# Order of the wide and narrow products inside a weight unit of the gated feed-forward blocks

## The chip, the cores and the metric

One Trainium2 chip, one core of it. The metric is the device time of one execution of the whole program in microseconds. The kernel before takes 1206.65 us (median of 3 runs, 1206.61 to 1206.96).

## What is computed

A chain of two small models on 256 tokens of width 1024, all in 32-bit floats. The part that the change touches is the gated feed-forward block (`swiglu`), which occurs four times, with a hidden width of 2816:

```python
D_FF = 2816
def swiglu(x, w_gu, w_down):
    gate, up = jnp.split(x @ w_gu, 2, axis=-1)
    return (jax.nn.silu(gate) * up) @ w_down

# layer of type A; the layer of type B has the same two feed-forward blocks
x = x + 0.5 * swiglu(rms_norm(x, ffn1_norm[l]), ffn1_w_gu[l], ffn1_w_down[l])
...
x = x + 0.5 * swiglu(rms_norm(x, ffn2_norm[l]), ffn2_w_gu[l], ffn2_w_down[l])
```

The program calls the four blocks a1, a2 (the two of layer A), b1 and b2 (the two of layer B). Everything else (a first model with attention and pooling, a gated delta rule, latent attention, norms) is left as it is.

## The kernel before

Activations lie transposed, 128 features on the partitions and 256 tokens in a row, so x is KC = 8 chunks of 128x256. Weights stream in from memory once, in slabs of two units. A unit of the up stage is 128 output features: eight pieces of 128x128, one for each chunk k. Each weight and each activation is split in a high and a low part: ScalarE writes `w_hi` from `raw` (`split_hi`, L576), VectorE writes `w_lo` = raw - w_hi (`split_lo`, its subtraction is L1120), and a product is high x high + low x high + high x low. Both rings hold four units (RING = 4).

In the up stage a unit is done by `project_halves` (L2104 on). For chunk k it issues two matmuls: one with the stationary piece `w_hi` and 512 moving columns, the high and the low part of the activations side by side (L2110, into all 512 columns of the unit's bank), and one with the stationary piece `w_lo` and the 256 high columns (L2112, added to the lower half of the same bank). So a unit is 8 pairs of a 512-column and a 256-column product, 16 matmuls, in the order 512, 256, 512, 256 and so on. Each matmul has a weight load of its own. TensorE waits at the unit's start for the semaphore of `w_lo` (`unit_begin`, L2087) and for a free bank (`bank_of`); the last matmul of the unit counts `unit_used` up (`unit_end`). That one signal frees the ring place for ScalarE (`slot` in the scalar block) and releases the readers of the bank: ScalarE copies the upper half out (`take_low`, L772), VectorE adds the lower half (`both_halves`, L1451), multiplies by the norm, and `silu`, gate product and a new split for the down stage follow (L785, L1484, L792).

`ffn(which)` holds the up stage. Its function `turn` does four units; the first turn of each block is written out with its own waits (`first` is given), and a loop on the engine (`Fori`) does the rest: 10 turns of 4 units in each of the four blocks (for b1 two pairs of units were done ahead). The down stage after it has its own code (`down`, L2419 and L2421) in the same 512, 256 order. The first turn of a2, b1 and b2 goes through `enter` (L2129, L2131). The trace shows 1328 matmuls each of L2110 and L2112.

SyncE issues the weight transfers by slab, four slabs ahead (RAW = 4), with waits on the ring.

Of the kernel before, what the change touches and what calls it, by code (L numbers as in the profile page):

```python
# [16 lines left out]
KC = D // P  # L17
SEQ = 256
# [139 lines left out]
def program(nc, dram, out):  # L158
    with ExitStack() as ctx:
# [7 lines left out]
        xs, _ = place("xs", at + 32, [P, KC, 2, SEQ], F32R)  # L167
        xs_hi, xs_lo = xs[:, :, 0], xs[:, :, 1]
# [5 lines left out]
        w_hi, at = place("w_hi", at, [P, RING, UNIT], F32R)  # L174
        w_lo, at = place("w_lo", at, [P, RING, UNIT], F32R)
# [180 lines left out]
        xh_ready, xg_ready = sem("xh_ready"), sem("xg_ready")  # L356
# [61 lines left out]
        def piece(tensor, u, b, n=1):  # L418

            return tensor[:, u % RING, b * P:(b + n) * P]  # L420
# [1653 lines left out]
        def _(pe):  # L2074
            def bank_of(t, off=0):

                if t >= 4:
                    pe.wait_ge(evac, t - 3 + off)
                return main[t % 4]
# [21 lines left out]
                    ins = triple(dst, piece(w_hi, u, k), piece(w_lo, u, k), hi[:, k], lo[:, k], k == 0, k == KC - 1)  # L2101
                unit_end(ins)

            def project_halves(u, bank, off=0, first=None):  # L2104

                unit_begin(u, off)
                for k in range(KC):
                    if first is not None:
                        pe.wait_ge(xg_ready, first + k + 1)
                    pe.matmul(bank[:, :], piece(w_hi, u, k), xs[:, k], start=k == 0, stop=k == KC - 1,  # L2110
                              skip_group_check=True)
                    ins = pe.matmul(bank[:, 0:SEQ], piece(w_lo, u, k), xs_hi[:, k], start=False, stop=k == KC - 1,  # L2112
                                    skip_group_check=True)
                unit_end(ins)

            def enter(u, banks, parts, first, late=1, norm=None, ready=xg_ready):
# [137 lines left out]
            for i in range(11):  # L2254
                ins = pe.matmul(side[1][:, 0:P], acc[:, 0:P], acc[:, 0:P], start=True, stop=True)
            ins.then_inc(warmed, 1)
            bank = side[2]
            pe.wait_ge(small_lo, 1)
            for k in range(KC):
                pe.wait_ge(xg_ready, k + 1)  # L2260
                w = slice(k * 8, k * 8 + P)
                ins = triple(bank[:, 0:TOK], wf_hi[:, w], wf_lo[:, w], xg_hi[:, k, :], xg_lo[:, k, :],
                             k == 0, k == KC - 1)
# [3 lines left out]
            t0 = FIRST_TILE["in1"]  # L2267
            for u in range(40):
# [6 lines left out]
                if u == POOL_AT:  # L2275
                    pe.wait_ge(pool_split, 1)
                    for j in range(2):
                        unit_begin(first_unit("w_pool") + j)
                        for i in range(2):
                            g = 2 * j + i  # L2280
                            ins = triple(pool_tile(g), piece(w_hi, first_unit("w_pool") + j, i),
                                         piece(w_lo, first_unit("w_pool") + j, i),
                                         pool_hi[:, g, :], pool_lo[:, g, :], True, True)
                        unit_end(ins)
                if 8 <= u < 12:

                    j = u - 8
# [4 lines left out]
                    for i, tok in enumerate((0, META, META + P)):  # L2292
                        for kk in range(2):
                            k = 2 * j + kk
                            x_t = slice(tok, tok + P)
                            ins = triple(main[(t0 + 8 + i) % 4][:, :], xg_hi[:, k, x_t], xg_lo[:, k, x_t],
                                         piece(w_hi, u, 4 * kk, 4), piece(w_lo, u, 4 * kk, 4),
                                         k == 0, k == KC - 1)
                    unit_end(ins)
                else:  # L2300
                    first = 0 if 4 <= u < 8 or 16 <= u < 20 else META
                    bank = bank_of(t0 + (u if u < 8 else u - 1))
# [3 lines left out]
                    if u == 0:  # L2306
                        pe.wait_ge(half_lo, 1)
                        for k in range(KC):
                            if k == KC // 2:
                                unit_begin(u)  # L2310
                            ins = triple(bank[:, 0:SEQ], piece(w_hi, u, k), piece(w_lo, u, k),
                                         xg_hi[:, k, META:TOK], xg_lo[:, k, META:TOK], k == 0, k == KC - 1)
# [3 lines left out]
                if u == 4:  # L2316

                    pe.wait_ge(rstd_ready, 1)
                    for j, (tok, n) in enumerate(((0, META), (META, P), (META + P, P))):
                        ins = pe.matmul(side[0][0:n, j:j + 1], rstd[:, tok:tok + n], ident[:, 0:1],  # L2320
                                        start=True, stop=True)
# [13 lines left out]
            t0, u0 = FIRST_TILE["up"], first_unit("w_up")  # L2335
# [50 lines left out]
            def ffn(which):  # L2386
                f, u0, t0 = FFNS.index(which), first_unit("w_gu_" + which), FIRST_TILE["gu_" + which]

                def turn(i, first=None):
                    if first is not None and which != "a1":  # L2390
                        enter(u0, [bank_of(t0 + j) for j in range(2)], (xs_hi, xs_lo) if which == "b2" else (xs,), first,
                              2 if which == "b2" else 1, None if which == "b2" else FFN_NORM[which])
                    for j in range(2 if first is not None and which != "a1" else 0, 4):
                        if which == "b2" and first is not None:
                            project(u0 + j, bank_of(t0 + j)[:, 0:SEQ], xs_hi, xs_lo,
                                    within=(KC - 2, lambda: norm_sum(FFN_NORM[which])) if j == 2 else None)
                        else:
                            project_halves(u0 + j, bank_of(t0 + j, i * 4), i * 4, first if j == 0 else None)
                        if first is not None and which == "a1" and j == 0:
                            norm_sum(FFN_NORM[which])  # L2400

                if which != "b1":
                    turn(0, XG0["ffn_" + which])
                with pe.Fori(0 if which == "b1" else 1, (FT - FFN_FIRST[which]) // 2) as i:
                    turn(i)
                u0, t0 = first_unit("w_down_" + which), FIRST_TILE["down_" + which]

                def down(m, i=0, joined_parts=True):
                    bank = bank_of(t0 + m, i * 4)
                    for j in range(2):  # L2410
                        u = u0 + 2 * m + j
                        pe.wait_ge(h_ready, f * FT + FT // 2 + j * (FT // 2 - 2))
                        unit_begin(u, i * 8)
                        for b in range(FT // 2):
                            k = j * (FT // 2) + b
                            if k >= FT - 2:
                                pe.wait_ge(h_ready, f * FT + k + 1)
                            if joined_parts:
                                pe.matmul(bank[:, :], piece(w_hi, u, b), h_both[:, :, k, :], start=k == 0,  # L2419
                                          stop=k == FT - 1, skip_group_check=True)  # L2420
                                ins = pe.matmul(bank[:, 0:SEQ], piece(w_lo, u, b), h_hi[:, k, :], start=False,  # L2421
                                                stop=k == FT - 1, skip_group_check=True)
                            else:
                                ins = triple(bank[:, 0:SEQ], piece(w_hi, u, b), piece(w_lo, u, b),
                                             h_hi[:, k, :], h_lo[:, k, :], k == 0, k == FT - 1)
                        unit_end(ins)

                if which == "b2":
                    for m in range(KC):
                        down(m, joined_parts=m < KC - 1)  # L2430
                else:
                    with pe.Fori(0, 2) as i:
                        for m in range(4):
                            down(m, i)
# [588 lines left out]
```

## Time and profile before

| | |
|---|---|
| median of the runs | 1206.65 us |
| the profiled execution | 1206.3 us, its span (first to last instruction) 1204.5 us |
| TensorE busy | 1194.0 us, 99% of the span, 7964 matmuls |
| TensorE weight loads | 1100.7 us, 91% |
| VectorE / ScalarE / GpSimd busy | 935.3 / 728.0 / 88.4 us |
| L2110, the 512-column products of the up stages | 1328, 461.1 us |
| L2112, the 256-column products of the up stages | 1328, 374.5 us |
| read from memory | 207.86 MB, 173 GB/s over the span |

Matmuls overlap in the pipeline: a 512-column one is shown 390 ns long and a 256-column one 282 ns, though the next one starts well before these have passed. What TensorE needs for a matmul is therefore the distance from its start to the next one's start, called its step below. It is read from the timeline, best over many matmuls.

### The profile page before, as it was taken

To read this page: it belongs to the slowest core of one execution; us is meant where nothing else is said; L and a number is where in the kernel's file an instruction comes from. 1 tells how busy PE (TensorE), PEld (TensorE's weight loads), DVE (VectorE), ACT (ScalarE), POOL (GpSimd) and SP (SyncE) were. 2 spreads that over 40 slices of the span, in tenths; PEclk is the share of its full clock that TensorE was granted. 3 is DMA by queue.
4 is the path that set the end of the run, shared out by engine and by line. 5 is a ranking of instruction groups with operands and counts; after the bars stand their busy time and mean duration, and the time that the engine had idled before them with its cause. 6 is when DMAs were issued, how large, how long until landed. Compare 5 with 4: busy or idle time off the path is not lost.

```text
span 1204.5 us, 22407 instructions
## 1 busy us (share of the span) xinstructions
PE 1194.0 (99%) x7964; PEld 1100.7 (91%) x7964; DVE 935.3 (78%) x1620; ACT 728.0 (60%) x1197; POOL 88.4 (7%) x104
## 2 busy tenths in 40 slices
PE   9999999999999999999999999999999999999998
PEld 8899999988888999999888889988888999888887
DVE  7576788988876789778888867888876777888853
ACT  6455656666654589467666556666654566666642
POOL 4851000000000001610000000000000000000000
PEclk9999999999999999999999999999999999999999
DMA  8444555655664445104555743555664423555730
GB/s 325 179 141 152 210 208 175 208 186 205 206 234 153 140 167 163 66 36 167 186 205 178 256 164 121 205 193 180 227 233 141 139 100 126 190 203 181 257 124 36
DMA packets 47993, 209.87 MB, mean 174 GB/s; under 512 B 3351, under 2 KB 4773, under 8 KB 43445
## 3 DMA queue, kind: packets, MB, share of 16 engines
q1 hardware_dynamic: 46720, 204.96, 48.2%
q10 hardware_dynamic: 1204, 4.01, 0.9%
q8 instruction: 41, 0.67, 0.2%
q14 instruction: 28, 0.22, 0.0%
HBM read 207.86 MB, written 1.10 MB: 173 GB/s over the span
## 4 chain that ended last, share of the span: by engine, by line
PE 92%; DVE 4%; ACT 2%; issue 1%; DMA 0%; DVEq 0%; ACTq 0%
PE main L2110 25%; PE main L2112 13%; PE main L2419 13%; PE main L2083 8%; PE main L2084 8%; PE main L2085 8%; PE main L2421 7%; DVE w_lo L1120 2%; DVE cy L1574 1%; PE side L2216 1%; PE main L2578 1%; PE main L2462 1%; PE side L2190 1%; PE main L2753 1%; PE main L2755 1%
## 5 line engine op out<-in xcount | busy, mean ns | idle before, releaser
L1120 DVE TENSOR_TENSOR w_lo<-raw,w_hi 128x1024 fp32r<-128x1024 f32 (+3 forms) x365 | 467.0, 1287 | 8.3 <-ACT w_hi L576 7.2
L2110 PE MATMUL main<-xs,w_hi 128*128 128x512 f32 x1328 | 461.1, 390 | 1.3 <-DVE w_lo L1120 0.8
L576 ACT ACTIVATE w_hi<-raw 128x1024 fp32r<-128x1024 f32 (+2 forms) x363 | 402.4, 1110 | 79.1 <-PE main L2085 59.0
L2112 PE MATMUL main<-xs,w_lo 128*128 128x256 f32 x1328 | 374.5, 282 | 0.0
L2110 PEld LDWEIGHTS main<-xs,w_hi 128*128 128x128 f32 x1328 | 249.2, 188 | 54.0 <-DVE w_lo L1120 1.8
L2112 PEld LDWEIGHTS main<-xs,w_lo 128*128 128x128 f32 x1328 | 251.0, 189 | 0.0
L2419 PE MATMUL main<-h_both,w_hi 128*128 128x512 f32 x682 | 236.6, 390 | 0.0
L2421 PE MATMUL main<-h_both,w_lo 128*128 128x256 f32 x682 | 192.3, 282 | 0.0
L2419 PEld LDWEIGHTS main<-h_both,w_hi 128*128 128x128 f32 x682 | 128.0, 188 | 26.8
L2421 PEld LDWEIGHTS main<-h_both,w_lo 128*128 128x128 f32 x682 | 128.9, 189 | 0.0
L2083 PE MATMUL main<-xs,w_hi 128*128 128x256 f32 x368 | 105.5, 287 | 0.4 <-DVE w_lo L1120 0.3
L2084 PE MATMUL main<-xs,w_lo 128*128 128x256 f32 x368 | 102.8, 279 | 0.0
L2085 PE MATMUL main<-xs,w_hi 128*128 128x256 f32 x368 | 102.6, 279 | 0.0
L2083 PE MATMUL main<-xg,w_hi 128*128 128x256 f32 (+1 forms) x288 | 83.8, 291 | 0.0
L2084 PE MATMUL main<-xg,w_lo 128*128 128x256 f32 (+1 forms) x288 | 81.0, 281 | 0.0
L2085 PE MATMUL main<-xg,w_hi 128*128 128x256 f32 (+1 forms) x288 | 81.0, 281 | 0.0
L1451 DVE TENSOR_TENSOR hid<-main,hid 128x256 f32<-128x256 f32 x84 | 35.6, 424 | 52.7 <-ACT hid L772 52.7
L772 ACT ACTIVATE hid<-main 128x256 f32<-128x256 f32 x84 | 32.1, 382 | 71.4 <-PE main L2112 71.3
L594 ACT ACTIVATE xs<-x,par 128x256 fp32r<-128x256 f32 (+1 forms) x48 | 23.9, 507 | 77.6 <-DVE x L1421 67.1
L2083 PEld LDWEIGHTS main<-xs,w_hi 128*128 128x128 f32 x368 | 69.2, 188 | 1.0 <-issue 0.7
L2084 PEld LDWEIGHTS main<-xs,w_lo 128*128 128x128 f32 x368 | 69.2, 188 | 0.1
L2085 PEld LDWEIGHTS main<-xs,w_hi 128*128 128x128 f32 x368 | 69.2, 188 | 0.0
(478 smaller groups left out, 1884.7 us busy)
## 6 DMA issues: line engine op xcount, KB each, us to landing
raw<-in_w_gu_a SPq DMA_DIRECT2D x44, 1024.0 KB, 5.1
raw<-in_w_gu_b SPq DMA_DIRECT2D x44, 1024.0 KB, 5.1
raw<-in_w_down_a SPq DMA_DIRECT2D x16, 1408.0 KB, 6.0
raw<-in_w_down_b SPq DMA_DIRECT2D x16, 1408.0 KB, 6.0
raw<-in_w_in SPq DMA_DIRECT2D x15, 1024.0 KB, 7.6
raw<-in_w_in_a SPq DMA_DIRECT2D x13, 1024.0 KB, 5.2
raw<-in_w_gates SPq DMA_DIRECT2D x4, 1024.0 KB, 5.2
raw<-in_w_up SPq DMA_DIRECT2D x4, 1024.0 KB, 5.2
```

The source lines that it names most:

```text
L576: act.activation(w_hi[:, u % RING, 0:n], raw[:, s % RAW, u % 2, 0:n], ACT.Copy).then_inc(hi_ready, 1)
L594: act.activation(dst, src, ACT.Copy, scale=g).then_inc(xh_ready, 1)
L772: act.activation(dst, main[(t0 + n) % 4][:, SEQ:2 * SEQ], ACT.Copy).then_inc(low_half, 1)
L1120: return dve.tensor_tensor(dst, src, hi.bitcast(F32), ALU.subtract)
L1451: dve.tensor_tensor(dst, main[(t0 + n) % 4][:, 0:SEQ], dst, ALU.add).then_inc(evac, 1)
L2083: pe.matmul(dst, a_hi, b_hi, start=first, stop=False)
L2084: pe.matmul(dst, a_lo, b_hi, start=False, stop=False)
L2085: return pe.matmul(dst, a_hi, b_lo, start=False, stop=last)
L2110: pe.matmul(bank[:, :], piece(w_hi, u, k), xs[:, k], start=k == 0, stop=k == KC - 1, skip_group_check=True)
L2112: ins = pe.matmul(bank[:, 0:SEQ], piece(w_lo, u, k), xs_hi[:, k], start=False, stop=k == KC - 1, skip_group_check=True)
L2419: pe.matmul(bank[:, :], piece(w_hi, u, b), h_both[:, :, k, :], start=k == 0, stop=k == FT - 1, skip_group_check=True)
L2421: ins = pe.matmul(bank[:, 0:SEQ], piece(w_lo, u, b), h_hi[:, k, :], start=False, stop=k == FT - 1, skip_group_check=True)
```

## The change

`project_halves` gets a parameter `group`. The chunks are walked in groups: in a group first all 512-column products are issued, then all 256-column ones. With group 1 the order is the one before. Block a1 gets 2, a2 gets 8 (the whole unit), b1 gets 4, b2 gets 1; the turn that is written out with `first` keeps 1. The number of matmuls, their operands, all waits and signals stay.

```diff
-            def project_halves(u, bank, off=0, first=None):
+            def project_halves(u, bank, off=0, first=None, group=1):
 
                 unit_begin(u, off)
-                for k in range(KC):
-                    if first is not None:
-                        pe.wait_ge(xg_ready, first + k + 1)
-                    pe.matmul(bank[:, :], piece(w_hi, u, k), xs[:, k], start=k == 0, stop=k == KC - 1,
-                              skip_group_check=True)
-                    ins = pe.matmul(bank[:, 0:SEQ], piece(w_lo, u, k), xs_hi[:, k], start=False, stop=k == KC - 1,
-                                    skip_group_check=True)
+                for k0 in range(0, KC, group):
+                    for k in range(k0, k0 + group):
+                        if first is not None:
+                            pe.wait_ge(xg_ready, first + k + 1)
+                        pe.matmul(bank[:, :], piece(w_hi, u, k), xs[:, k], start=k == 0, stop=k == KC - 1,
+                                  skip_group_check=True)
+                    for k in range(k0, k0 + group):
+                        ins = pe.matmul(bank[:, 0:SEQ], piece(w_lo, u, k), xs_hi[:, k], start=False, stop=k == KC - 1,
+                                        skip_group_check=True)
                 unit_end(ins)
...
-                            project_halves(u0 + j, bank_of(t0 + j, i * 4), i * 4, first if j == 0 else None)
+                            project_halves(u0 + j, bank_of(t0 + j, i * 4), i * 4, first if j == 0 else None,
+                                           {"a1": 2, "a2": KC, "b1": 4, "b2": 1}[which] if first is None else 1)
```

## Rows read from the trace of the kernel before

**Rows 1.** The page: busy time of the engines, and TensorE's granted clock in 40 slices.
```profile
PE 1194.0 (99%) x7964; PEld 1100.7 (91%) x7964; DVE 935.3 (78%) x1620; ACT 728.0 (60%) x1197; POOL 88.4 (7%) x104
...
PEclk9999999999999999999999999999999999999999
```

**Rows 2.** The page: the chain that ended last, shares by engine and by line.
```profile
PE 92%; DVE 4%; ACT 2%; issue 1%; DMA 0%; DVEq 0%; ACTq 0%
PE main L2110 25%; PE main L2112 13%; PE main L2419 13%; PE main L2083 8%; PE main L2084 8%; PE main L2085 8%; PE main L2421 7%; DVE w_lo L1120 2%; DVE cy L1574 1%; PE side L2216 1%; PE main L2578 1%; PE main L2462 1%; PE side L2190 1%; PE main L2753 1%; PE main L2755 1%
```

**Rows 3.** Busy time by stretch, in the loops of a1, a2, b1, b2; clock, DMA last.
```profile
core 0: us, PE busy (x) PEld busy (x) DVE busy (x) ACT busy (x) POOL busy (x), PEclk, DMA share, GB/s
225.00:340.00 115.00, 115.00 (x665) 101.94 (x665) 97.81 (x170) 73.83 (x126) 0.00 (x0) 1.00 0.59 204
575.00:685.00 110.00, 110.00 (x637) 97.53 (x636) 94.03 (x162) 70.84 (x120) 0.00 (x0) 1.00 0.58 205
775.00:885.00 110.00, 110.00 (x637) 97.49 (x636) 92.09 (x157) 70.56 (x120) 0.00 (x0) 1.00 0.58 205
1030.00:1140.00 110.00, 110.00 (x637) 97.53 (x636) 94.35 (x161) 72.00 (x121) 0.00 (x0) 1.00 0.58 205
```

**Rows 4.** Waits between engines, 225 to 340 us: total us, times, longest.
```profile
ACT hid L772 <- PE main L2112: 17.2, 18, 1.0
DVE hid L1451 <- ACT hid L772: 13.5, 19, 0.8
ACT h_both L792 <- DVE hid L1484: 13.1, 21, 0.8
ACT gate_n L772 <- PE main L2112: 7.2, 18, 0.4
```

**Rows 5.** TensorE's timeline in block a1, pairs: start us, length us, instruction.
```profile
300.04 0.39 PE L2110 MATMUL main<-xs,w_hi 128*128 128x512 f32 x1
300.27 0.28 PE L2112 MATMUL main<-xs,w_lo 128*128 128x256 f32 x1
300.39 0.39 PE L2110 MATMUL main<-xs,w_hi 128*128 128x512 f32 x1
...
340.60 0.39 PE L2110 MATMUL main<-xs,w_hi 128*128 128x512 f32 x1
```

**Rows 6.** TensorE's timeline, first model: 512-column products in one row.
```profile
35.63 0.39 PE L2083 MATMUL main<-w_hi,xg 128*128 128x512 f32 x1
35.86 0.39 PE L2084 MATMUL main<-w_hi,xg 128*128 128x512 f32 x1
...
38.88 0.40 PE L2085 MATMUL main<-w_lo,xg 128*128 128x512 f32 x1
39.11 0.40 PE L2083 MATMUL main<-w_hi,xg 128*128 128x512 f32 x1
39.35 0.40 PE L2084 MATMUL main<-w_hi,xg 128*128 128x512 f32 x1
...
52.16 0.40 PE L2085 MATMUL main<-w_lo,xg 128*128 128x512 f32 x1
```

**Rows 7.** TensorE's timeline: first and last of 47 256-column products, activations moving.
```profile
429.59 0.28 PE L2084 MATMUL main<-xs,w_lo 128*128 128x256 f32 x1
...
434.96 0.28 PE L2085 MATMUL main<-xs,w_hi 128*128 128x256 f32 x1
```

**Rows 8.** TensorE's timeline: first and last of 47 256-column products, weights moving.
```profile
212.90 0.28 PE L2084 MATMUL main<-w_hi,mem_lo 128*128 128x256 f32 x1
...
218.35 0.28 PE L2085 MATMUL main<-w_lo,mem_hi 128*128 128x256 f32 x1
```

**Rows 9.** TensorE's weight loads beside the pair of Rows 5: start us, length us.
```profile
300.05 0.19 PEld L2112 LDWEIGHTS main<-xs,w_lo 128*128 128x128 f32 x1
300.27 0.19 PEld L2110 LDWEIGHTS main<-xs,w_hi 128*128 128x128 f32 x1
300.39 0.19 PEld L2112 LDWEIGHTS main<-xs,w_lo 128*128 128x128 f32 x1
```

**Rows 10.** TensorE's timeline in block a2: the wait for w_lo inside the up stage.
```profile
571.11 0.28 PE L2112 MATMUL main<-xs,w_lo 128*128 128x256 f32 x1
572.22 0.50 PE L2110 MATMUL main<-xs,w_hi 128*128 128x512 f32 x1 [0.83 <-DVE w_lo L1120]
```

## The prediction

> **What bounds the kernel now.** I read the page first: TensorE is busy for 99% of the span, at the full granted clock in all 40 slices [rows 1]. The chain that ended last is TensorE for 92%, and the two lines that the change reorders, L2110 and L2112, are 25% and 13% of it, the largest share of any two lines [rows 2]. Busy time is a weak witness for TensorE, since its matmuls overlap, so I read the loops of the four blocks by stretch: TensorE has no idle time at all in them, VectorE is busy for 97.81 of 115 us, ScalarE for 73.83, and the DMA engines for 0.59 of the time, at 204 GB/s; b2's stretch looks like the others [rows 3]. The waits say the same from the other side: in the loop of a1 ScalarE and VectorE wait for L2112's end and for each other, and no wait of TensorE is among the four longest [rows 4]. The only stall of TensorE of that kind that I found inside an up stage's loop is one in a2, 0.83 us, for the first `w_lo` after the entry [rows 10]. So the time of an up stage is the number of matmuls times their steps, and whatever the new order does to a step goes straight to the end.
>
> The step now: from 300.04 to 340.60 us lie 117 pairs of a 512-column and a 256-column product [rows 5], 40.56 us, so 346.7 ns for a pair. The single starts give about 0.23 us for the 512 and 0.12 us for the 256 [rows 5]. This average over 117 pairs includes fourteen unit boundaries, so a boundary adds nothing that shows.
>
> **The change, part by part.** *Matmuls, weight loads, signals.* None is added or taken away. The waits stand where they stood, at the unit's start; `unit_used` still comes from the last matmul of the unit, a 256-column one as before. The queues of SyncE, ScalarE, VectorE and GpSimd are not touched, and no DMA is moved. The pieces of `w_lo` are read later in the unit, but they are still waited for at its start, so nothing is won at the stall of 0.83 us [rows 10]. The upper half of the bank is finished earlier, by up to seven 256-column products in a2, but its reader waits for `unit_used` and gains nothing. Cost of all this: nothing. If a step does grow, VectorE and ScalarE only wait longer; if it shrinks, VectorE has 115 - 97.81 = 17 us of cover in that stretch, 15% [rows 3], far more than a step can shrink.
>
> *Neighbours.* What does change is which product stands beside which. In a group of g chunks, g - 1 times a 512-column product is followed by a 512-column one instead of by a 256, and g - 1 times a 256 is followed by a 256 instead of by a 512. Call one such couple a join. A unit has 4 joins in a1 (four groups of 2), 7 in a2 (one group of 8), 6 in b1 (two groups of 4) and none in b2. Each block has 10 turns of 4 units in its loop, 40 units, so 40 x (4 + 7 + 6) = 680 joins among 960 pairs of 120 units. The time moves by 680 times the difference between (step of a 512 among 512s + step of a 256 among 256s) and 346.7 ns.
>
> *A 256 among 256s.* 47 of them in a row, with the activations `xs` moving as here, start from 429.59 to 434.96 us: 5.37 us over 46 steps, 116.7 ns [rows 7]. With the weights as the moving operand it is 5.45 over 46, 118.5 ns [rows 8]. I take 116.7, since the operands are those of the change; the other is the upper end.
>
> *A 512 among 512s.* The change's own case, `xs` moving in a row of 512s, is not in the trace. The nearest is the first model's row of 72, where the weights move and the activations are stationary: from 35.63 to 52.16 us are 71 steps, 16.53 us, 232.8 ns [rows 6]. It is not even: two steps from 38.88 to 39.35 take 0.47 us, 235 ns each, and the first one, 35.63 to 35.86, takes 0.23 [rows 6]. A 256-column product loses 118.5 - 116.7 = 1.8 ns when the weights are what moves [rows 7, 8]; I take that off once and get 231.0 ns for `xs` moving. The upper end is 235. The lower end is further away. In the pairs 256 more columns cost 0.23 - 0.12 = 0.11 us [rows 5], so 512 columns by themselves are worth about 220 ns, and if standing in a row took away all that comes on top, 220 would be the step. Nothing excludes it, so it stays an end of the range. The loads say little either way: each starts with the matmul ahead of its own (300.27 beside the matmul of 300.27), is shown 0.19 us long, and the next matmul starts 0.12 us after it began [rows 5, 9]; beside a 512 a load has more room than that, so two 512s in a row can't wait for a load.
>
> *The sum.* 231.0 + 116.7 = 347.7 ns against 346.7, so +1.0 ns for a join and 680 x 1.0 = +0.7 us. The profiled execution took 1206.3 us (its span 1204.5 and 1.8 around it), which gives 1207.0; the median of the runs lies 0.35 us higher, so 1207.35 there. By block that is +0.16 us in a1, +0.28 in a2 and +0.24 in b1, too little to be seen in any of them except by counting steps. With the ends: 232.8 + 116.7 = 349.5 gives +1.9 us (1208.6), which is the case that the row of 512s holds as it stands; 228 + 116.7 = 344.7, where a 512 keeps the step that it has in the pairs (346.7 less 118.5 is 228.2), gives -1.4 us (1205.3). These three are one case to me: no order matters by more than 3 ns for a join.
>
> A measurement of this kernel can tell about 0.2% from no change, 2.4 us here, which is 3.5 ns for a join.
>
> **The rivals.** *A, the row of equal widths runs free.* If what a 512-column step has on top of its columns comes from the change of width, it goes in a row: 220 + 116.7 = 336.7, -10.0 ns for a join, -6.8 us, 1199.9. For it speaks that a 256 among 256s is 1 or 2 ns shorter than beside a 512 [rows 5, 7]; against it, that the 72 equal 512s of the first model never get near 220 [rows 6]. For the same end there is a rule of the Trainium skill, page "TensorE: Matmul & The Clock Gate", section "Back-to-back issue gap": columns divided by 2.4 GHz plus 2.5 ns at the full clock. That would make 215.8 and 109.2, 325.0 for a pair, and by it the sum for 680 joins would be -14.8 us; the pairs here take 346.7, so this trace does not agree with it for the order of before, and for the order of after it is one more reason to leave A a chance.
>
> *B, the row of equal widths is the slower rhythm.* In the mixed order the stretch 512, 256 takes less than the sum of its parts from the two uniform rows (346.7 against 232.8 + 116.7 = 349.5). If that is a matter of rhythm, that a load beside a 256 and the reading of the next moving columns catch up with each other only when widths alternate, then the first 512s of a group settle, as in the first model, from 0.23 to 0.235 [rows 6], and the 256s behind them don't gain: 235 + 118.5 = 353.5, +6.8 ns for a join, +4.6 us, 1211.2. It counts as slower from 3.5 ns for a join. For it speaks the uneven row of 512s, whose later steps are longer; against it that such a row has another moving operand, and that 256s in a row do gain. The Trainium skill says in the same page, section "Step-by-step: what each phase is for", that loading the next weights does not steal read bandwidth from the running matmul; by that no order could cost anything and B would be +0. The trace can't show it, as no matmul here runs without a load beside it.
>
> *C, nothing happens.* The step of a pair is set by its 768 columns and two loads, whatever stands beside them: 346.7 as before, 1206.65. It can't be told from the forecast in the total, only in the steps.
>
> **How the numbers follow.** The forecast and C lie together between 1205.3 and 1208.6 and hold 0.62. A, in full or in part, has 0.18: only a step of a kind that the trace does not have would bring it. B, in full or in part, has 0.20. The range reaches into both, to leave about one in ten outside at each end: below, 1203.5 is -4.6 ns for a join, a 512 at 225.4 with a 256 at 116.7 (680 x -4.6 = -3.1 us from the median); above, 1210.5 is +5.7 ns for a join (+3.9 us). The predicted time is 1207.35, given as 1207.4. Chances: faster by over 0.2% 0.18, within it 0.62, slower 0.20.
>
> **What the changed kernel's profile would show.** Right, if the pairs in b2's loop still take 346.7 ns; if in a2's loop (from about 575 us) a unit of eight 512s and eight 256s takes 2.77 to 2.79 us, with starts of the 512s 0.23 us apart and of the 256s 0.12; if TensorE still has no idle time in the loops and the waits on L2112's end by ScalarE are as long as now. A would show 512s 0.22 us apart and a2's loop about 2.8 us shorter, most of all blocks, as it has 7 of the 17 joins of each set of units. B would show steps of 0.235 and more, and a2 longer by about 1.9 us. Wrong altogether would be the count of joins if the loss or gain were not in the proportion 4 : 7 : 6 between a1, a2 and b1, or if b2 moved too; wrong would also be the claim on signals if a stall of TensorE appeared at a unit's start that isn't there now.

## The result and the profile after

The changed kernel takes 1208.85 us (median of 19 executions, 1208.4 to 1209.47) against 1206.55 for the kernel before (19 executions, 1206.33 to 1206.96): +2.3 us, ratio 1.0020, 95% interval 1.0013 to 1.0026. The profiled execution took 1208.72 us, its span is 1206.9.

The page of the changed kernel, busy time, chain by engine, and the two lines (L2111 and L2114 are the L2110 and L2112 of before):

```profile
PE 1196.0 (99%) x7964; PEld 1098.0 (91%) x7964; DVE 935.7 (78%) x1620; ACT 728.2 (60%) x1197; POOL 88.3 (7%) x104
...
PE 91%; DVE 5%; ACT 2%; issue 1%; DMA 1%; DVEq 0%; SPq 0%; ACTq 0%
...
L2111 PE MATMUL main<-xs,w_hi 128*128 128x512 f32 x1328 | 395.8, 393 | 1.3 <-DVE w_lo L1120 0.8
L2114 PE MATMUL main<-xs,w_lo 128*128 128x256 f32 x1328 | 261.5, 280 | 0.0
```

The same two lines on the page of the kernel before:

```profile
L2110 PE MATMUL main<-xs,w_hi 128*128 128x512 f32 x1328 | 461.1, 390 | 1.3 <-DVE w_lo L1120 0.8
L2112 PE MATMUL main<-xs,w_lo 128*128 128x256 f32 x1328 | 374.5, 282 | 0.0
```

Beside [rows 1, 2] and these nearly all is the same: as many instructions, as much idle time ahead of the two lines (1.3 and 0.0 us). Their busy time falls from 461.1 and 374.5 to 395.8 and 261.5 us, which is no gain: matmuls of one line that overlap are merged when they are neighbours. The page doesn't tell where 2.3 us went. The stretches inside the four loops do, by their counts (columns as in [rows 3]):

```profile
225.00:340.00 115.00, 115.00 (x666) 101.43 (x665) 97.79 (x170) 73.64 (x127) 0.00 (x0) 1.00 0.58 203
575.00:685.00 110.00, 110.00 (x632) 95.64 (x631) 93.30 (x159) 69.84 (x121) 0.00 (x0) 1.00 0.58 205
777.00:887.00 110.00, 110.00 (x629) 95.52 (x629) 91.18 (x157) 69.81 (x119) 0.00 (x0) 1.00 0.58 204
1032.00:1142.00 110.00, 110.00 (x636) 97.55 (x635) 94.32 (x162) 71.97 (x122) 0.00 (x0) 1.00 0.58 205
```

TensorE is busy without a gap in all of them, at the full granted clock, before and after. But in 110 us it starts 632 matmuls in a2 and 629 in b1, where it started 637 before [rows 3]; in a1 (115 us) and b2 they are 666 and 636, within one of the 665 and 637 of before. So the loss lies in a2 and b1, in the steps and not in waits. TensorE's timeline gives the steps. Where matmuls of one line follow each other, a row merges them; its start is that of the first of them. First a1 (groups of 2), then a2 (8), b1 (4) and b2 (1):

```profile
300.22 0.62 PE L2111 MATMUL main<-xs,w_hi 128*128 128x512 f32 x2
300.67 0.40 PE L2114 MATMUL main<-xs,w_lo 128*128 128x256 f32 x2
...
340.43 0.62 PE L2111 MATMUL main<-xs,w_hi 128*128 128x512 f32 x2
...
600.51 2.03 PE L2111 MATMUL main<-xs,w_hi 128*128 128x512 f32 x8
602.38 1.09 PE L2114 MATMUL main<-xs,w_lo 128*128 128x256 f32 x8
...
662.11 2.03 PE L2111 MATMUL main<-xs,w_hi 128*128 128x512 f32 x8
...
800.63 1.09 PE L2111 MATMUL main<-xs,w_hi 128*128 128x512 f32 x4
801.57 0.63 PE L2114 MATMUL main<-xs,w_lo 128*128 128x256 f32 x4
...
860.84 1.09 PE L2111 MATMUL main<-xs,w_hi 128*128 128x512 f32 x4
...
1100.07 0.39 PE L2111 MATMUL main<-xs,w_hi 128*128 128x512 f32 x1
...
1133.69 0.39 PE L2111 MATMUL main<-xs,w_hi 128*128 128x512 f32 x1
```

- a1: 58 groups of two, 116 pairs, in 340.43 - 300.22 = 40.21 us: 346.6 ns a pair. Nothing lost.
- a2: 22 units, 176 pairs, in 662.11 - 600.51 = 61.60 us: 350.0 ns a pair. Eight 512s take 1.87 us; over the whole loop, by the trace's unrounded starts, a 512 takes 233.3 and a 256 116.7.
- b1: 43 groups of four, 172 pairs, in 860.84 - 800.63 = 60.21 us: 350.1 ns a pair.
- b2: 97 pairs in 33.62 us: 346.6 ns.

320 pairs of a2 and 320 of b1 at 3.33 ns more each make +2.13 us of the 2.3. The rest, about 0.2 us, lies ahead of the loops of a2 and b1 in the profiled execution: the wait in a2 of [rows 10] ends at 572.40 instead of 572.22, before any group of more than two has run. The first 222 us of the program, which no experiment here touches, vary by as much and more: over the traces of this document the first up-stage product of a1 starts between 221.35 and 222.17 us. The row in a2 shows the same wait as before:

```profile
572.40 2.13 PE L2111 MATMUL main<-xs,w_hi 128*128 128x512 f32 x8 [0.83 <-DVE w_lo L1120]
```

### The profile page after: what moved, and what is told of

Same layout as the page of the kernel before. It is cut to its first block, busy times and chain, and to the rows that moved or that the text cites. A ratio compares the mean times of both kernels' runs of the same rounds, so it can differ in the third digit from the quotient of the medians.

```text
span 1206.9 us, 22407 instructions
## 1 busy us (share of the span) xinstructions
PE 1196.0 (99%) x7964; PEld 1098.0 (91%) x7964; DVE 935.7 (78%) x1620; ACT 728.2 (60%) x1197; POOL 88.3 (7%) x104
## 4 chain that ended last, share of the span: by engine, by line
PE 91%; DVE 5%; ACT 2%; issue 1%; DMA 1%; DVEq 0%; SPq 0%; ACTq 0%
PE main L2111 25%; PE main L2114 13%; PE main L2422 13%; PE main L2083 8%; PE main L2084 8%; PE main L2085 8%; PE main L2424 7%; DVE w_lo L1120 2%; DVE cy L1574 1%; PE side L2218 1%; PE main L2581 1%; PE main L2465 1%; PE side L2192 1%; PE main L2756 1%; PE main L2758 1%
## 5 line engine op out<-in xcount | busy, mean ns | idle before, releaser
L2111 PE MATMUL main<-xs,w_hi 128*128 128x512 f32 x1328 | 395.8, 393 | 1.3 <-DVE w_lo L1120 0.8
L2114 PE MATMUL main<-xs,w_lo 128*128 128x256 f32 x1328 | 261.5, 280 | 0.0
L2111 PEld LDWEIGHTS main<-xs,w_hi 128*128 128x128 f32 x1328 | 229.7, 188 | 34.5 <-DVE w_lo L1120 1.8
L2114 PEld LDWEIGHTS main<-xs,w_lo 128*128 128x128 f32 x1328 | 221.2, 188 | 24.3
L2084 PE MATMUL main<-xs,w_lo 128*128 128x256 f32 x368 | 102.9, 280 | 0.0
L2083 PEld LDWEIGHTS main<-xs,w_hi 128*128 128x128 f32 x368 | 69.2, 188 | 1.0 <-issue 0.7
L2084 PEld LDWEIGHTS main<-xs,w_lo 128*128 128x128 f32 x368 | 69.3, 188 | 0.1
L2085 PEld LDWEIGHTS main<-xs,w_hi 128*128 128x128 f32 x368 | 69.2, 188 | 0.0
```

The source lines that it names most:

```text
L2083: pe.matmul(dst, a_hi, b_hi, start=first, stop=False)
L2084: pe.matmul(dst, a_lo, b_hi, start=False, stop=False)
L2085: return pe.matmul(dst, a_hi, b_lo, start=False, stop=last)
```

## The experiments

Two theories stood against each other after this. J is the prediction's: every couple of equal neighbours costs a little. R, for rhythm (a sequence of steps that repeats through a whole loop): only the order of widths matters, groups of two cost nothing and longer rows cost the same 3.3 ns for every pair, however many changes of width are left. `ORDER` is a table that I put in the place of the argument `group`; W is a 512-column product, n a 256-column one; runs(2, 2, 2, 2) is four groups of two, runs(8) one of eight.

**e1_two_all**

```diff
-{"a1": 2, "a2": KC, "b1": 4, "b2": 1}[which] if first is None else 1
+{"a1": 2, "a2": 2, "b1": 2, "b2": 2}[which] if first is None else 1
```

> Groups of two in the loops of all four blocks (the changed kernel has them in a1 only). In the changed kernel's trace the loop of a1 keeps 346.7 ns for a pair of a 512- and a 256-column product, the loops of a2 (rows of eight) and b1 (rows of four) take 350. Theory R (rhythm: only long rows of one width are slow, groups of two are free): 0.0 us, ratio 1.000 to the kernel before, 346.7 ns for a pair in all four loops. Theory J (each couple of equal neighbours costs, as in the prediction): 160 units x 4 joins = 640 joins; with the 2.14 us that a2 and b1 lost spread over the 680 joins of the changed kernel, 3.15 ns each, +2.0 us, ratio 1.0017.

Measured: median 1208.44 against 1206.55, ratio 1.0013 (1.0004 to 1.0022; the ratios are those on record and can differ by a few ten-thousandths from the quotient of the medians), but the eleven executions don't stand around that median: four took 1206.5 to 1206.9 and seven took 1208.4 to 1208.9. The profiled one was of the first kind and had all four loops at 346.7, as R says. J's +2.0 us fits the second kind only by chance, as e8 below shows.

**e2_eight_all**

```diff
-{"a1": 2, "a2": KC, "b1": 4, "b2": 1}[which] if first is None else 1
+{"a1": KC, "a2": KC, "b1": KC, "b2": KC}[which] if first is None else 1
```

> One group of eight (all 512-column products of a unit, then all its 256-column ones) in the loops of all four blocks, 160 units. Theory R: every pair costs 350.0 instead of 346.7 ns, 160 x 8 x 3.35 = +4.3 us over the kernel before, ratio 1.0036, the same loss of 1.07 us in each block. Theory J: 160 x 7 = 1120 joins x 3.15 = +3.5 us, ratio 1.0029. A theory by which the loss is nothing but the spread between traces: under +1 us.

Measured: 1211.04 against 1206.55 us, ratio 1.0038 (1.0024 to 1.0051), +4.5 us, five executions within 0.45 us. R gave +4.3, J +3.5; the interval of the ratio, some +2.9 to +6.2 us, holds both, so the steps decide. J's 3.15 ns for a join would be 349.4 ns a pair. In the trace the loops of a1 and b1 take 350.0 ns a pair and those of a2 and b2 350.8, which makes 2 x 1.07 + 2 x 1.33 = +4.8 us; the profiled execution, the longest of the five at 1211.39, is 4.8 above the median of before. So double the dose costs double, and a loop can stand a little above 350 too.

**e3_patterns**

```diff
+ORDER = {
+    "a1": runs(3, 3, 2),
+    "a2": [(kind, (k + 4 * (kind == "n")) % KC) for k in range(KC) for kind in "Wn"],
+    "b1": pattern("WWWWnnWWnnWWnnnn"),
+    "b2": [("W", k) for k in range(KC)] + [("n", k) for k in reversed(range(KC))],
+}
```

> Four orders in one kernel, one for each block's loop; what is read is the step in each loop, W a 512-column product, n a 256-column one. a1: groups of 3, 3 and 2. a2: widths alternate as before, but the 256-column product behind chunk k is that of chunk (k + 4) mod 8, so weights and moving columns of neighbours are no longer of the same chunk. b1: WWWWnnWWnnWWnnnn, rows of four only at the ends of the unit. b2: a row of eight 512s, then the eight 256s in reverse order of chunks. Theory R (the widths' order alone decides, groups over two are slow): a1 2800 ns for a unit if three is already too long, else between 2773 and 2800; a2 2773; b1 between, as its middle is groups of two; b2 2800. Theory O (what counts is that a chunk's two products stand together, the same 256 moving columns twice): a2 2800, b2 2800. Theory J: a1 5 joins, 2790; a2 none, 2773; b1 8 couples of 512s and 256s less the mixed ones, about 5 joins, 2790.

Measured, per pair in each loop: a1 350.8 ns, a2 346.7, b1 348.3, b2 350.8 (a unit is eight times that: 2807, 2773, 2787, 2807). The total was 1209.67 us. TensorE's timeline of a2 in this kernel, two pieces of it:

```profile
600.17 0.39 PE L2140 MATMUL main<-xs,w_hi 128*128 128x512 f32 x1
600.40 0.28 PE L2143 MATMUL main<-xs,w_lo 128*128 128x256 f32 x1
...
660.49 0.39 PE L2140 MATMUL main<-xs,w_hi 128*128 128x512 f32 x1
```

174 pairs in 60.32 us, 346.7 ns, though the two neighbours are of chunks four apart. Theory O (the chunk's two products must stand together) falls, and J with it: a1 has 5 joins and loses as much as b2 with 7. Rows of three are already too long, and the group of two beside them doesn't run free either: its 512s take 231 to 234 ns. In b1 a 512 takes 233.3 ns in the row of four that opens the unit and 228.0 in the groups of two in the middle; the unit loses 13 ns, half of what a unit of long rows loses, on average 348.3 a pair.

**e4_one_width**

```diff
+ORDER = {
+    "a1": by_chunk("W", "L"),   # L: w_lo against all 512 columns
+    "a2": by_row("W", "L"),
+    "b1": by_chunk("h", "n"),   # h: w_hi against the 256 high columns
+    "b2": by_row("h", "n"),
+}
```

> Sixteen products of one width in each unit, to separate width from weights. a1: both products of a chunk 512 columns wide, loads of w_hi and w_lo taking turns (this adds the low x low part). a2: the same, first the eight with w_hi, then the eight with w_lo. b1: only 256 columns for w_hi too (this leaves out the high x low part), w_hi and w_lo taking turns. b2: the same, eight w_hi and then eight w_lo. Theory R (width alone): a1 and a2 both 233.3 ns a product, b1 and b2 both 116.7. Theory H (the faster step of the order before comes from w_hi and w_lo taking turns at the load): a1 near 228.3 and b1 near 116 or less, a2 233.3 and b2 116.7. The total is of no interest: a1 and a2 are longer by 16 x 233.3 - 2773 = 960 ns a unit, some 77 us for both, and b1 and b2 shorter until the weights' transfer is what they wait for.

The timeline of its a1, where `w_hi` and `w_lo` take turns at 512 columns:

```profile
299.66 0.40 PE L2132 MATMUL main<-xs,w_hi 128*128 128x512 f32 x1
299.90 0.39 PE L2132 MATMUL main<-xs,w_lo 128*128 128x512 f32 x1
...
302.46 0.40 PE L2132 MATMUL main<-xs,w_hi 128*128 128x512 f32 x1
```

Twelve steps in 2.80 us, 233.3 ns, and over the whole loop 233.3 as well, in a2 the same. Theory H falls: it is not the turn of `w_hi` and `w_lo` at the load that gives 228 ns, but the turn of widths. It also gives the number that the prediction lacked: with `xs` moving a 512 among 512s takes 233.3 ns. In b1 and b2 TensorE waited for VectorE's `w_lo` at unit after unit, so their mean step says nothing; with the steps that hold a wait left out, a 256 takes 117.1 ns where `w_hi` and `w_lo` take turns (b1) and 117.2 in rows (b2), so at 256 columns too the turn of the weights makes no difference. The total, 1249.91 us, is that of more work and not a comparison.

**e8_two_again**, the kernel of e1 unchanged, to catch the other kind of execution.

> The kernel with groups of two in all four blocks once more, unchanged. Its executions fell in two clusters, 1206.5 to 1206.9 and 1208.4 to 1208.9, and the profile that was taken was of the first (1206.7), with 346.7 ns for a pair in all four loops. If the groups of two can run in the slower rhythm too, a profiled execution near 1208.7 shows loops with more than 346.7 ns for a pair: two of the four loops at 350.0 (2 x 1.07 = +2.1 us), or all four at 348.3. If the second cluster comes from somewhere else (a start, a stall), all four loops stay at 346.7 and the 2.1 us lie elsewhere. A profile of the first cluster again leaves it open.

The profiled execution was of the second kind, 1208.58 us. Median of eight 1208.62 against 1206.5, ratio 1.0015 (1.0004 to 1.0027); one of the eight was at 1206.88, the others from 1208.4 on. TensorE's timeline, first in a1, then in a2:

```profile
300.07 0.62 PE L2135 MATMUL main<-xs,w_hi 128*128 128x512 f32 x2
300.53 0.40 PE L2138 MATMUL main<-xs,w_lo 128*128 128x256 f32 x2
300.76 0.62 PE L2135 MATMUL main<-xs,w_hi 128*128 128x512 f32 x2
...
572.26 0.73 PE L2135 MATMUL main<-xs,w_hi 128*128 128x512 f32 x2 [0.83 <-DVE w_lo L1141]
...
574.48 0.63 PE L2135 MATMUL main<-xs,w_hi 128*128 128x512 f32 x2
574.96 0.40 PE L2138 MATMUL main<-xs,w_lo 128*128 128x256 f32 x2
575.19 0.64 PE L2135 MATMUL main<-xs,w_hi 128*128 128x512 f32 x2
...
672.71 0.64 PE L2135 MATMUL main<-xs,w_hi 128*128 128x512 f32 x2
```

and the same stretch in the profiled execution of e1, which took 1206.68 us:

```profile
574.02 0.62 PE L2135 MATMUL main<-xs,w_hi 128*128 128x512 f32 x2
574.48 0.40 PE L2138 MATMUL main<-xs,w_lo 128*128 128x256 f32 x2
574.72 0.62 PE L2135 MATMUL main<-xs,w_hi 128*128 128x512 f32 x2
...
668.32 0.62 PE L2135 MATMUL main<-xs,w_hi 128*128 128x512 f32 x2
```

It is the same program on the same data, and a2's loop runs in another rhythm, from its first group to its last: 139 groups, 278 pairs, in 98.23 us are 353.3 ns a pair in e8, and 136 groups, 272 pairs, in 94.30 us are 346.7 in e1. The other three loops take 346.7 in both. 320 x 6.67 = 2.13 us, which is the distance of the two clusters. So a steady order of products can run in more than one steady rhythm, and a loop keeps the one it is in.

Where the rhythm is picked isn't shown. The two traces of a2 differ from the first group behind the wait of 0.83 us on: behind the first two 512s, e8's steps are 120, 115, 238, 234 ns and again, while e1's come to 117, 120, 227, 229 within two groups. TensorE enters b2's loop behind idle time as well, and those of a1 and b1 without any. From the trace of the kernel before, at b2's first product:

```profile
1024.07 0.49 PE L2110 MATMUL main<-xs,w_hi 128*128 128x512 f32 x1 [0.49 <-DVE gate_n L1249]
```

An order has been seen at two rates in one and the same loop in a2 alone: groups of two at 346.7 and 353.3, and rows of eight at 350.0 in the changed kernel and 350.8 in e2 and e11.

**e5_columns_rows** and **e6_columns_turns** cut the wide products to 320, 384, 448 and 480 columns, one width for each block, once in rows of eight and once taking turns.

```diff
+e5: ORDER = {"a1": by_row("W", "n", 320), "a2": by_row("W", "n", 384), "b1": by_row("W", "n", 448), "b2": by_row("W", "n", 480)}
+e6: ORDER = {"a1": by_chunk("W", "n", 320), "a2": by_chunk("W", "n", 384), "b1": by_chunk("W", "n", 448), "b2": by_chunk("W", "n", 480)}
```

> The row of eight in each loop, with the wide products cut to fewer columns: 320 in a1, 384 in a2, 448 in b1, 480 in b2 (this leaves out a part of the high x low sum, so it is only for reading steps). In rows, 256 columns take 116.7 ns and 512 take 233.3. Theory P (in a row a column costs the same however many there are, 0.456 ns): 145.8, 175.0, 204.2, 218.8 ns. Theory F (full rate of one column in 1/2.4 ns and a fixed part of 20 ns at 512): 153, 180, 207, 220 ns; it does not fit the 116.7 of 256 columns, where the fixed part would be 10. Theory Q (the step only takes certain lengths): steps from 256 to 512 in jumps, two neighbouring column counts alike.

> The order of the kernel before (wide and narrow taking turns), with the wide products cut as in the kernel for rows: 320 columns in a1, 384 in a2, 448 in b1, 480 in b2. At 512 columns the pair takes 346.7 ns, 3.3 less than 233.3 + 116.7 of the uniform rows. Theory R (any mix of widths saves about 3 ns a pair over rows): pairs of 259, 288, 317.5 and 332 ns, if rows go in proportion. Theory S (only 512 beside 256 happens to fit): the saving differs from width to width or is gone, pairs of 262.5, 291.7, 320.8, 335.4.

Mean steps of a wide product and of a pair in the loops, from the unrounded starts, over 270 to 320 products of each kind (512: the changed kernel's a2 and the kernel before). With 320 and 384 columns TensorE waited for `w_lo` at unit starts, in both orders alike (a1's products span 102.47 us in both kernels, a2's 101.18 and 101.19). The steps that hold such a wait are left out; at 384 columns some are hard to tell from the others, so its pairs are good to about 0.5 ns:

| columns | wide, in rows | wide, taking turns | pair, in rows | pair, taking turns |
|---|---|---|---|---|
| 320 | 146.4 | 145.7 | 263.8 | 263.3 |
| 384 | 175.0 | 174.5 | 292.1 | 291.7 |
| 448 | 203.8 | 202.7 | 320.8 | 320.0 |
| 480 | 216.8 | 217.2 | 334.2 | 333.3 |
| 512 | 233.3 | 228.3 | 350.0 | 346.7 |

Theory P is within 1% in rows, F is out by 4 to 5% at 320 and Q falls too: the steps grow all the way. For the turns R is wrong and S right, its pairs within 0.7%: from 320 to 480 columns taking turns saves 0.4 to 0.9 ns, and the 3.3 ns are there only at 512. The two totals, single executions of 1162.32 and 1161.81 us, differ by 0.5 us, as the table would have it for b1 and b2 (2 x 320 x 0.8 ns); in the two traces each of these loops differs by 0.25 to 0.27 us. So "taking turns is faster" is no rule; the full width of 512 beside 256 is the case that gains by it.

**e7_two_banks**

```diff
+TWO_UNITS = {
+    "a1": [(kind, j, k) for k in range(KC) for j in range(2) for kind in "Wn"],
+    "a2": [(kind, j, k) for k in range(KC) for kind in "Wn" for j in range(2)],
+    "b1": [(kind, j, k) for kind in "Wn" for k in range(KC) for j in range(2)],
+    "b2": None,
+}
```

> Two units at a time, so that neighbours can go to different banks of the accumulator: a1 W n of one unit, W n of the other, chunk by chunk; a2 W of both, then n of both; b1 rows of sixteen W and sixteen n, banks taking turns; b2 as before. Theory B (the time over the columns' own comes from adding into the same bank again and again): with banks changing from product to product a2 and b1 fall, towards 325 to 335 ns for a pair. Theory R (widths alone): a1 346.7, a2 346.7 (groups of two), b1 350, whatever the bank, b2 346.7.

The total is 1398.52 us: two units are freed together and TensorE waits for `w_lo` in every couple of units, two of its waits stand below, and the granted clock falls to half in stretches behind them (0.958 on average). That is the cost of the edit, not of banks. The steps inside can still be read; the timeline of b1, banks changing from product to product:

```profile
970.73 3.76 PE L2158 MATMUL main<-xs,w_hi 128*128 128x512 f32 x15 [2.19 <-DVE w_lo L1146]
974.34 2.03 PE L2161 MATMUL main<-xs,w_lo 128*128 128x256 f32 x16
976.20 0.40 PE L2158 MATMUL main<-xs,w_hi 128*128 128x512 f32 x1
978.78 5.31 PE L2158 MATMUL main<-xs,w_hi 128*128 128x512 f32 x15 [2.18 <-DVE w_lo L1146]
```

Sixteen 256s take 1.87 us by the unrounded starts, 116.7 each. Inside the row of 512s one starts at 971.30 and one at 973.87, eleven steps in 2.57 us, 233.6 each. With a new bank for each product both steps are those of one bank, and Theory B falls. Over all of b1's loop at the full granted clock, steps with a wait left out, a pair takes 349.6 ns (Theory R 350, Theory B 325 to 335), a1's 346.9 and a2's 349.0; R had 346.7 for a2, but two or three groups behind every wait are longer there.

The last four experiments take single blocks apart, all against 33 executions of the kernel before (median 1206.59, 1206.34 to 1207.29), 11 of each.

**e9_two_a2**: `ORDER = {"a2": runs(2, 2, 2, 2)}`, the other blocks as before.

> Groups of two in the loop of a2 alone, the other three blocks as before. With groups of two in all blocks, the profiled execution of 1206.7 us had 346.7 ns for a pair in all four loops, that of 1208.6 us had 353.3 in the whole loop of a2 and 346.7 in the others: 40 x 8 x 6.67 ns = 2.13 us. Theory L (a loop falls into one of several steady rhythms when it is entered, and a2, entered behind a wait of 0.83 us for w_lo, falls into either): two clusters again, 1206.5 and 1208.65, nothing between. Theory M (the other loops have a part in it): other values, or one cluster.

Measured: 1206.59, 1206.3 to 1207.0, ratio 1.0000 (0.9991 to 1.0009): one cluster, none of the 11 near 1208.6, no loss. In e1 and e8, 14 of 19 executions had the slower rhythm, and a2's entry is the same in all three. Theory M fits this and Theory L as it was put doesn't, but it isn't shown that the other blocks have a part in it: e1, e8 and e9 ran on three different chips (7 of 11 slower on e1's, 7 of 8 on e8's), and the kernel of e1 never ran on e9's.

**e10_mixed_a2**: `ORDER = {"a2": runs(1, 1, 2, 2, 2)}`, the other blocks as before.

> Only the loop of a2 is changed: in each unit the first two chunks in the order of before (W n W n), the other six in three groups of two. Theory L with a pull (products of changing width bring the rhythm back to 346.7): no second cluster, 1206.5 in all executions. Theory L without a pull (what the loop is entered with stays): two clusters, the second one at most 3/4 of 2.13 us above, 1208.1, or higher if the first two chunks take part.

Measured: 1207.14, 1206.71 to 1207.8, ratio 1.0004 (0.9995 to 1.0013). Neither case of the expectation: one cluster, but a2's whole loop takes 348.3 ns a pair in the trace. The first products of two of its units:

```profile
600.06 0.39 PE L2135 MATMUL main<-xs,w_hi 128*128 128x512 f32 x1
...
661.36 0.39 PE L2135 MATMUL main<-xs,w_hi 128*128 128x512 f32 x1
```

61.30 us for 22 units, 176 pairs. That makes 320 x 1.67 = +0.53 us; the median is 0.55 higher, though the interval of the ratio holds no change as well, so it is the trace that shows the loss. Two orders that can run free by themselves were not free when they alternated, and Theory R in its simple form (groups of two free, longer rows not) doesn't hold here.

**e11_eight_a2**, `ORDER = {"a2": runs(8)}`, and **e12_four_b1**, `ORDER = {"b1": runs(4, 4)}`, are the two costly parts of the change, each alone.

> The row of eight in the loop of a2 alone: one part of the change. From the traces, where this loop takes 350.0 ns a pair in the changed kernel and 350.8 where all four blocks have rows of eight: 320 pairs x 3.33 to 4.17 = +1.07 to +1.33 us, 1207.6 to 1207.9, one cluster. Theory J (joins, as predicted): 280 x 1.0 = +0.3 us.

> Groups of four in the loop of b1 alone: the other part. 320 pairs x 3.33 ns = +1.07 us, 1207.6. Theory J as predicted: 240 x 1.0 = +0.24 us. If it is nearer to 0 than to 1, the loss of the changed kernel is not the sum of its parts.

Measured: e11 1207.94 (1207.46 to 1208.24), e12 1207.93 (1207.27 to 1208.17), both ratio 1.0010 (1.0001 to 1.0019), +1.35 and +1.34 us; the prediction had +0.28 and +0.24 for these two. In e11's trace a2's loop has, first and last row of 22 units:

```profile
600.60 2.03 PE L2135 MATMUL main<-xs,w_hi 128*128 128x512 f32 x8
...
662.35 2.03 PE L2135 MATMUL main<-xs,w_hi 128*128 128x512 f32 x8
```

61.75 us for 176 pairs are 350.9 ns, +1.33 us for the loop, as measured. b1's loop in e12 takes 350.0, which gives +1.07, and its median has 0.3 us more. The profiled execution (1208.13 us) has more than that ahead of the first product of a1's up stage, in the kernel before and in e12:

```profile
221.49 0.59 PE L2110 MATMUL main<-xs,w_hi 128*128 128x512 f32 x1
...
222.17 0.59 PE L2135 MATMUL main<-xs,w_hi 128*128 128x512 f32 x1
```

That is 0.68 us in a part that the edit doesn't touch; with the 1.07 us of b1's loop it is all but 0.1 us of the 1.8 between the two spans (1204.5 and 1206.3). Whether the other executions of e12 had the same there, no trace tells. Each part alone costs over half of what both cost together in the changed kernel (2.3), so the sum of the parts, 2.7 us, is the whole within some 0.4 us, of which the traces place 0.27: a2's loop takes 350.0 in the changed kernel and 350.8 in e11.

## Why the prediction was right, and where it was not

The time came out inside the range and on the boundary of what was called no change, +2.3 us where 2.4 was the bound. The median lies 1.45 us above the predicted 1207.4; of the loss of 2.3 us the forecast had 0.7. The median also lies above the 1208.6 at which the forecast's own stretch ended, so that the time was right by a narrow margin, and two of the signs that the prediction named for itself did not come: a unit in a2 takes 2.80 us where it had 2.77 to 2.79, and the loss is not in the proportion 4 : 7 : 6.

- **That steps alone set the time: right.** No wait changed, b2 did not move, TensorE stayed without idle time in the loops, and ScalarE's longest wait for the unit's end by `hid` is 1.0 us in a1 and a2, before and after.
- **The step of a 256 among 256s, 116.7 ns: right.** e7 and the changed kernel have 116.7. In other rhythms it is not quite that: 117.6 in the rows of eight of e2 and e11 in a2.
- **The step of a 512 among 512s, 231.0 ns: wrong, 233.3 (e4, and the changed kernel).** The failed step is the discount of 1.8 ns for the moving operand. Two rows of 256s differ by it [rows 7, 8], and I carried it over to 512s, where it does not exist. Nor is it shown that the moving operand makes it at 256: rows of eight 256s with the same operands differ by 0.8 ns in a2's loop (116.8 in the changed kernel, 117.6 in e11). The 2.3 ns too few are 680 x 2.3 = 1.6 us, the whole distance from +0.7 to +2.3. The row of 72 in the first model as it stood, 232.8 [rows 6], was the better witness: its case, 349.5 for a pair and 1208.6 us, was named and came within 0.25 us of the result.
- **The count of 680 joins: wrong as an account.** The 4 joins of a unit in a1 cost 0, the 6 in b1 and the 7 in a2 cost the same 27 ns a unit. The pattern 4 : 7 : 6 that would have shown the account right was in truth 0 : 1 : 1. It had let a1 bear a quarter of the cost, and made the cost smaller where it fell: by joins a2 would have needed +3.8 ns for each, b1 +4.4. A price for neighbours also can't say why the last 512 of a row of four, which a 256 follows as in the order of before, takes 233 ns there and 228 before; or why in a1's groups of two the first 512 takes 227 ns and the first 256 117.5, less than the 228.3 and 118.3 of before, and the second ones 229 and 120, which gives it back. That 680 joins at the right step, 350.0 - 346.7, come to 2.3 us is luck: the loss goes by the 640 pairs of a2 and b1, and 640 is near 680.
- **Rival B** had the right place and sign: the mixed order saves by its rhythm, and a uniform one settles near the first model's row (233.3 and 232.8). It was given 0.20; what was forecast with 0.62, no order worth more than 3 ns for a join, was out where the cost fell (+3.8 and +4.4). Its price (+4.6 us) assumed that the 256s don't gain, and they do. What it says of weight loads catching up with the reading of moving columns was tested by nothing; e4 shows only that it is not a matter of which weights are loaded, e7 that it is not a bank. Why long rows settle in a slower rhythm stays open.
- **Rival A** found nothing: no step of a 512 below 225 ns in any loop of the changed kernel, and none nears 215.8. The formula of the Trainium skill ("TensorE: Matmul & The Clock Gate", "Back-to-back issue gap") is 12 to 20 ns too short for a 512 here and 7 to 10 for a 256, by the loops' means in every order. The same section gives it for an isolated matmul and not for a stream with a weight load before each, which is what runs here; the prediction leaves that condition out.

## What to carry to other kernels

Where TensorE has no idle time, an edit that only reorders matmuls is priced by steps, start to start over a hundred or more of them, and the time of the whole is then that difference times the count; the busy times on the page moved by 178 us for a loss of 2.3. Take the step from the row whose widths stand in the new order, even if its operands are others, and do not correct it by an effect seen at another width. Count what changes by loop or unit as well as by neighbours: a row's step can hold for the whole row and the loop. Look at each order's steps in every loop and in more than one execution: groups of two looked free in the trace and were 2.1 us slower in 14 of 19 executions.

## What the runs showed of the hardware

- The 3.3 ns a pair that the order of before has over uniform rows exist at 512 beside 256 columns (346.7 against 350.0); with 320, 384, 448 or 480 columns beside 256 it is under 1 ns.
- One order can have several steady rhythms: groups of two at 346.7 or 353.3 ns a pair in the same loop of the same program, rows of eight at 350.0 or 350.8 in different kernels and loops, each held to the loop's end. With groups of two in a2 alone the times of 11 executions have only the faster one; with all four blocks so, 14 of 19 have the slower. Whether the other blocks or the chip makes that difference stays open, and so does where the rhythms come from.
- In rows of one width a product of these 32-bit operands takes about 10 ns more than its columns at 2.4 GHz at 256 columns (116.7 against 106.7) and 20 ns more at 512 (233.3 against 213.3), whether the bank changes or not (e7) and whichever of `w_hi` and `w_lo` is loaded (e4).
- No order was found that beats 346.7 ns. Of the kernels that compute the whole result none is faster than the kernel before; groups of two in a2 alone (e9) are as fast.
